# A hybrid recurrent and attention block: the attention output projection by token halves, inputs scaled as they are split, the embedding projection moved, the score heads alternated

## What is computed

```
h = rmsnorm(x, g_mix);  z = h @ w_in            # lx, lg, q, k, v
y_lru = rmsnorm(rg_lru(conv(lx)) * gelu(lg), g_lru_out)
y_att = rmsnorm(chunk_window_attention(q, k, v, sinks), g_attn_out)
x = x + concat([y_lru, y_att]) @ w_out
h = rmsnorm(x, g_ffn)
x = x + square(relu(h @ w_ff1)) @ w_ff2         # d_ff = 4096
gate = sigmoid(rmsnorm(x, g_ple) @ w_ple_gate)
x = x + gate * (p @ w_ple_proj)                 # p is 1024 x 256
return rmsnorm(x, g_final)
```

## Time and profile before

| | |
|---|---|
| median of 3 runs | 1165.95 us (1165.94 to 1166.27) |
| the profiled execution | 1165.31 us |
| its span in the profile | 1163.5 us |
| mean granted TensorE clock | 0.987 of full |
| PE / DVE / ACT / POOL busy | 1120.2 / 690.1 / 363.8 / 397.4 us |

### The profile page before, as it was taken

How to read it: one execution, slowest core, us unless ns; L and a number is a source line. 1 busy time by engine, 2 the same in 40 slices (tenths; PEclk the granted TensorE clock), 3 DMA queues, 4 the chain that set the end, 5 groups by cost and what they waited for, 6 DMA issues and landing times.

```text
span 1163.5 us, 13983 instructions
## 1 busy us (share of the span) xinstructions
PE 1120.2 (96%) x5196; PEld 922.9 (79%) x5196; DVE 690.1 (59%) x869; ACT 363.8 (31%) x597; POOL 397.4 (34%) x207
## 2 busy tenths in 40 slices
...
DMA packets 22481, 69.43 MB, mean 60 GB/s; under 512 B 2352, under 2 KB 4400, under 8 KB 22448
## 3 DMA queue, kind: packets, MB, share of 16 engines
...
## 4 chain that ended last, share of the span: by engine, by line
PE 83%; DVE 12%; issue 2%; POOL 1%; ACT 1%; DMA 1%; SPq 0%; DVEq 0%; ACTq 0%
PE bank L460 27%; PE bank L461 26%; PE bank L462 26%; DVE h_lo L1042 4%; DVE r_mix L1047 1%; DVE xT L1271 1%; PE bank L550 1%; DVE lane L1094 1%; DVE scaled L1269 1%; PE bank L579 1%; POOL gx_lo L397 1%; PE bank L508 1%; PE bank L564 1%; DMA stage<-in_w_in 1%; POOL w_lo L368 1%
## 5 line engine op out<-in xcount | busy, mean ns | idle before, releaser
L460 PE MATMUL bank<-h_hi,w_hi 128*128 128x512 f32 (+1 forms) x1056 | 408.9, 387 | 25.2 <-DVE h_lo L1042 16.1
L461 PE MATMUL bank<-h_lo,w_hi 128*128 128x512 f32 (+1 forms) x1056 | 401.7, 380 | 0.0
L462 PE MATMUL bank<-h_hi,w_lo 128*128 128x512 f32 (+1 forms) x1056 | 401.4, 380 | 0.0
L430 POOL TENSOR_TENSOR w_lo<-stage,w_hi 128x1024 fp32r<-128x1024 f32 x64 | 152.7, 2409 | 524.6 <-ACT w_hi L940 524.6
L1319 DVE TENSOR_TENSOR xT<-bank,xT 128x512 f32<-128x512 f32 x256 | 176.3, 691 | 142.6 <-PE bank L462 142.3
L460 PEld LDWEIGHTS bank<-h_hi,w_hi 128*128 128x128 f32 x1056 | 201.7, 191 | 72.1 <-issue 10.2
L461 PEld LDWEIGHTS bank<-h_lo,w_hi 128*128 128x128 f32 x1056 | 202.0, 191 | 37.4 <-issue 1.6
L462 PEld LDWEIGHTS bank<-h_hi,w_lo 128*128 128x128 f32 x1056 | 201.5, 191 | 37.7
L460 PE MATMUL bank<-u_hi,w_hi 128*128 128x512 f32 x512 | 199.2, 389 | 0.0
L461 PE MATMUL bank<-u_lo,w_hi 128*128 128x512 f32 x512 | 199.2, 389 | 0.0
L462 PE MATMUL bank<-u_hi,w_lo 128*128 128x512 f32 x512 | 199.2, 389 | 0.0
...
## 6 DMA issues: line engine op xcount, KB each, us to landing
...
out_x<-o_ring SPq DMA_DIRECT2D x7, 256.0 KB, 2.2
...
```

The lines of the kernel that those rows point to most:

```text
L430: pool.tensor_tensor(w_lo[:, n0 % 2, o:o + HP], stage[:, s0 % STAGES, :], w_hi[:, n0 % 2, o:o + HP], ALU.subtract).then_inc(w_split, 1)
L460: pe.matmul(o, whi, hh, start=first, stop=False)
L461: pe.matmul(o, whi, hl, start=False, stop=False)
L462: return pe.matmul(o, wlo, hh, start=False, stop=last)
```

## The change

- **Score heads alternated.** `scores(u)` issued the four matmuls of key/value head 0 (channels on partitions 0 to 63, bank 4) and then the four of head 1 (partitions 64 to 127, bank 5). It now issues head 0, head 1, head 0, head 1, and both heads' outputs are signalled at the end.
- **Attention output projection by token halves.** Stage 3 now does all 8 output tiles of token half 0, then those of half 1, so both weight pieces are needed by the fifth group, and piece 9 is free only after group 12. 
- **Its inputs scaled when split.** `att_norm` (VectorE, one instruction per tile, L1159's form) multiplies attention outputs by gain and 1/rms; `att_high` copies (ScalarE), `att_low` subtracts (VectorE); `add_a` is one VectorE instruction. For this the sum of squares of half 0 is moved forward: GpSimd adds it after `probs(6)` and before `probs(7)`, ScalarE squares in unit 5, and TensorE's `sum_rows(SS_ATT)` stands in unit 6 behind `turn_p(6)` instead of behind unit 7's groups.
- **The feed-forward's inputs scaled when split.** `ffn_norm` (VectorE, 16 instructions) applies gain and 1/rms, `ffn_split` (ScalarE) copies, and the 16 subtractions move from VectorE to GpSimd (`ffn_low`). `hidden`'s relu no longer multiplies. VectorE adds the squares of half 1 (GpSimd did). The first `ff1` waits for the sum of squares, root and reciprocal of its token half; its half 1 goes by input tiles with both outputs in step. It waits for `main_free` A0+15 (bank 0, `add_a(14)`) and A0+16.
- **Embedding projection moved.** All 8 outputs of part 0 are computed right after the last `ff2`, ScalarE copies them to `kept` in SBUF, and the gates of part 0 follow without projections between them. The embedding weights come by two transfers on ScalarE's queue in stage 3 instead of through SyncE's stage ring, and are split by ScalarE and VectorE in the first feed-forward block instead of by ScalarE and GpSimd after the last.

```diff
             if n < IN_PIECES:
                 eng.wait_ge(main_done, 4 * (n + 1))
+            elif n < IN_PIECES + 2:
+                eng.wait_ge(main_done, L0 + 8 * (n - IN_PIECES + 1))
             else:
-                eng.wait_ge(main_done, IN_GROUPS + 8 * (n - IN_PIECES + 1))
+                eng.wait_ge(main_done, A0 + 12 + 4 * (n - IN_PIECES - 2))
...
+                if u == 6:
+                    sums(SS_ATT, sq, acc)
             low(2 * 10)
             low(2 * 10 + 1)
             sums(SS_FFN, sq, acc)
+
+            def ffn_low(k, hf):
+
+                pool.wait_ge(ffn_high, KD * hf + k + 1)
+                pool.tensor_tensor(h_lo[:, k, half(hf)], raw_h(k, hf), h_hi[:, k, half(hf)], ALU.subtract
+                                   ).then_inc(ffn_ready, 1)
+
+            for k in range(4):
+                ffn_low(k, 0)
             low(2 * FF_FIRST)
             low(2 * FF_FIRST + 1)
-            sums(SS_FFN + 1, sq, acc)
+            for k in range(4, KD):
+                ffn_low(k, 0)
+            for k in range(KD):
+                ffn_low(k, 1)
...
                 pe.wait_ge(main_free, IN_GROUPS - (0 if u >= UNITS // 2 else 2))
-                for g in range(NKV):
-                    if u >= 1:
-                        pe.wait_ge(s_read, 2 * (u - 1) + g + 1)
-                    else:
-                        pe.wait_ge(rms_done, SS_LRU + 2)
-                    r = slice(g * HD, (g + 1) * HD)
-                    for cp in range(2):
-                        c = 2 * u + cp
-                        for a in range(2):
+                if u >= 1:
+                    pe.wait_ge(s_read, 2 * u)
+                else:
+                    pe.wait_ge(rms_done, SS_LRU + 2)
+                for cp in range(2):
+                    c = 2 * u + cp
+                    for a in range(2):
+                        for g in range(NKV):
+                            r = slice(g * HD, (g + 1) * HD)
                             last = pe.matmul(bank[4 + g][:, (2 * cp + a) * P:(2 * cp + a + 1) * P],
                                              qT[r, c, 2 * a:2 * a + 2, :].rearrange("p a q -> p (a q)"),
                                              kT[r, c * CHUNK:c * CHUNK + P], start=True, stop=True)
-                    last.then_inc(s_done, 1)
+                            if cp == 1 and a == 1:
+                                last.then_inc(s_done, 1)
...
-                if u == UNITS - 1:
-                    pe.wait_ge(s_read, 2 * UNITS)
-                    sum_rows(SS_ATT, acc, 4)
+                        if u == UNITS - 2:
+                            pe.wait_ge(s_read, 2 * UNITS)
+                            sum_rows(SS_ATT, acc, 4)
                 values(u)
             for g in range(A_GROUPS):
-                n, hf, m = g // 8, (g % 8) // 4, g % 4
+                hf, n, m = g // 8, (g % 8) // 4, g % 4
                 if g == 3:
                     pe.wait_ge(o_read, UNITS)
                 group(A0 + g, IN_PIECES + 2 + n, LT, m, hf, LT, H_ATT + 4 * hf if n == 0 and m == 0 else None,
-                      g % 8 == 0)
-                if g == 4:
+                      hf == 0 and m == 0)
+                if g == 1:
                     sum_rows(SS_ATT + 1, acc, 5)
-                if g == 14:
+                if g == 8:
                     sum_rows(SS_FFN, acc, 7)
...
+            pe.wait_ge(w_split, 2 * (FF_FIRST + 1))
             for hf in range(2):
-                pe.wait_ge(h_ready, ffn_number(KD - 1, hf) + 1)
                 for m in range(2):
-                    pe.wait_ge(main_free, MAIN_GROUPS - 1 + hf)
-                    ff1(0, hf, m)
-                    if hf == 1 and m == 0:
+                    pe.wait_ge(relu_done, 2 * hf + m + 1)
+                pe.wait_ge(main_free, A0 + (15, 16)[hf])
+                for k, m in ([(k, m) for m in range(2) for k in range(KD)] if hf == 0 else
+                             [(k, m) for k in range(KD) for m in range(2)]):
+                    if m == 0:
+                        pe.wait_ge(ffn_ready, KD * hf + k + 1)
+                    c = k * 256 + m * P
+                    last = passes(bank[2 * hf + m][:, :], w_hi[:, n1, c:c + P], w_lo[:, n1, c:c + P],
+                                  h_hi[:, k, half(hf)], h_lo[:, k, half(hf)], k == 0, k == KD - 1)
+                    if k == KD - 1:
+                        last.then_inc(ff1_done, 1)
+                    if hf == 0 and m == 0 and k == 5:
                         sum_rows(SS_FFN + 1, acc, 7)
...
...
+            for m in range(KD):
+                project(0, m)
+            pe.wait_ge(y_added, 4 + 16 * FF_BLOCKS)
+            sum_rows(SS_PLE, acc2, 4)
             for part in range(len(PARTS)):
                 for i in range(GATE_PIECES):
                     for m in range(2):
                         gate(part, i, m)
-                        if part == 0 and i == 0 and m == 0:
-                            pe.wait_ge(y_added, 4 + 16 * FF_BLOCKS)
-                            sum_rows(SS_PLE, acc2, 4)
-                    for m in range(2):
-                        project(part, 2 * i + m)
+                    if part >= 1:
+                        for m in range(2):
+                            project(part, 2 * i + m)
...
+                if u == 5:
+                    for j in range(LT):
                         square(SQ_BY[SS_ATT] - 4 + j, sq, q_tile(j, 0))
-            root(SS_ATT, 4, r_mix, ATT)
+                if u == 6:
+                    root(SS_ATT, 4, r_mix, ATT)
+                if u == 7:
+                    att_high(0)
             act.wait_ge(o_read, UNITS)
-            for j in range(LT):
-                split_high(H_ATT + 4 + j, q_tile(j, 1), v_att[:, j:j + 1], LT + j, 1)
             for j in range(LT):
                 square(SQ_BY[SS_ATT + 1] - 4 + j, sq, q_tile(j, 1))
             piece_free(act, 8)
             high(2 * 10)
             high(2 * 10 + 1)
             root(SS_ATT + 1, 5, r_mix, ATT)
+
+            def ffn_split(k, hf):
+
+                act.wait_ge(ffn_normed, KD * hf + k + 1)
+                act.activation(h_hi[:, k, half(hf)], raw_h(k, hf), ACT.Copy).then_inc(ffn_high, 1)
+
+            def ffn_square(k, hf):
+                act.wait_ge(main_free, A0 + 8 * hf + k + 1)
+                square(SQ_BY[SS_FFN + hf] - 8 + k, sq, xT[:, k, half(hf)])
+
+            for k in range(2):
+                ffn_square(k, 0)
+            att_high(1)
             act.dma_start(pT[:, :, :], p.rearrange("(k q) t -> q k t", q=P)).then_inc(p_in, 16)
-
...
+            for k in range(2, KD):
+                ffn_square(k, 0)
+            act.wait_ge(h_ready, H_PLE)
+            for h in range(2):
+                act.dma_start(pw_raw[:, h * HP:(h + 1) * HP], w_ple_proj[0, h]).then_inc(pw_in, 16)
+            ffn_square(0, 1)
+            root(SS_FFN, 7, r_ffn, D)
+            ffn_square(1, 1)
             for k in range(4):
-                ffn_square(k, 0)
-                ffn_high(k, 0)
+                ffn_split(k, 0)
+                if k % 2 == 1:
+                    ffn_square(2 + k // 2, 1)
             piece_free(act, 9)
             high(2 * FF_FIRST)
             high(2 * FF_FIRST + 1)
-            for k in range(4):
-                ffn_high(k, 1)
             for k in range(4, KD):
-                ffn_square(k, 0)
-                ffn_high(k, 0)
-            for k in range(4):
+                ffn_split(k, 0)
+                if k == 5:
+                    ffn_square(4, 1)
+            for k in range(5, KD):
                 ffn_square(k, 1)
-            root(SS_FFN, 7, r_ffn, D)
-            for k in range(4, KD):
-                ffn_high(k, 1)
-                ffn_square(k, 1)
+            root(SS_FFN + 1, 7, r_ffn, D)
+            for k in range(KD):
+                ffn_split(k, 1)
...
+            def ple_high(k, hf):
+                act.wait_ge(y_added, 4 + 16 * (FF_BLOCKS - 1) + KD * hf + k + 1)
+                split_high(H_PLE + KD * hf + k, xT[:, k, half(hf)], v_ple[:, k:k + 1], k, hf)
+                square(SQ_BY[SS_PLE + hf] - 8 + k, sq2, xT[:, k, half(hf)])
+
+            def keep(m):
+                act.wait_ge(ple_done, m + 1)
+                act.activation(kept[:, m, :], bank[m % 4][:, :], ACT.Copy).then_inc(pp_kept, 1)
 
...
-            ple_high(0)
-            project_high()
+            for k in range(KD):
+                ple_high(k, 0)
+            keep(0)
+            keep(1)
             act.wait_ge(ff2_done, 16 * FF_BLOCKS)
-            gate_high(GATE_FIRST + 2)
+            gate_high(GATE_FIRST + 1)
+            for k in range(6):
+                keep(2 + k)
+                ple_high(k, 1)
             root(SS_PLE, 4, r_mix, D)
-            ple_high(1)
+            for k in range(6, KD):
+                ple_high(k, 1)
...
+            def att_norm(hf):
+
+                for j in range(LT):
+                    dve.wait_ge(sq_done, SQ_BY[SS_ATT + hf] - 3 + j)
```

(77 more changed lines are left out.)

124 lines of the change are left out of this document (57 added, 67 removed).

## The result

After the change the kernel takes 1171.76 us, the median of five runs (1171.3 to 1172.01), against 1165.95 before (five runs now, 1163.19 to 1167.52): 1.0051 of the time before, with a 95% interval of 1.0036 to 1.0066. It is slower, by 5.8 us; the forecast was 1162.5. The profiled execution took 1172.01 us with a span of 1170.2, 6.7 more than the span before.

What follows compares the result with a forecast made beforehand. TensorE, busy 96% of the span, was taken as the bound. Terms -3.2 + 4.5 + 1.7 + 3.9 - 10.3 = -3.4 on 1165.3 gave 1161.9, with 0.6 for the median 1162.5 us; range 1152 to 1172.

Steps and rivals of the forecast that it cites:

- The gates' part 0: Stretch after the last `ff2`: with projections moved ahead of the gates it falls from 66.9 to 56.6 us, -10.3 us.
- The wait for half 0's sum in unit 6: Attention unit 6: TensorE waits for ScalarE's squares and GpSimd's copy and adds of them, +4.5 us.
- everything moves together: Premise in attention unit 6: shorter scores shift all engines' work there alike, leaving the 4.5 us wait unchanged.
- The scores: Attention units: alternated heads share the array, 0.63 us less per group; five groups (scores 3 to 7) count, -3.2 us.
- rival B: Attention scores: the heads don't share the array, so the first edit does nothing; +3.2, 1165.7 us, chance 0.12.
- I count these two: Stage 3, half 0's chain: of 14 VectorE instructions only two meetings, with GpSimd's 1024-column weight lows, cost time: 4.4 us.
- The 47.3 without meetings: Stage 3: half 0's chain, through `add_a(14)`, ends at 47.3 us if no VectorE instruction meets GpSimd.
- GpSimd's short lows: Stage 3: 512-column lows come in pairs with gaps, partly over while ScalarE squares; no meetings with them counted.
- From half 1's sum to `ff2`: Feed-forward start: root, reciprocal, scaling, copy, eight GpSimd lows and two weight lows take 24.1 us, to `ff2` at 82.5.
- the term that stood at +3.9: Start of stage 3 to the first `ff2`: 82.5 us against 78.6, +3.9 us, bounds -5 and above +12.
- One loss of 1.7 us: Lower clock behind the new waits in unit 6 and ahead of `ff2`, counted once for both: +1.7 us (0 to 3.4).
- Rival A: Stage 3: VectorE and GpSimd take turns throughout, chain ends at 60, clock falls at both waits; 1172.3 us, chance 0.21.

## Why the prediction was wrong

The sum said 3.4 us less on the profiled execution, and it became 6.7 more, a miss of 10.1 us.

**Right.** The gates' part 0: -10.3 said, -10.6 measured, and the same 56.21 us when done alone. The wait for half 0's sum in unit 6: 4.5 said; TensorE stood still for 5.2 (252.96 to 258.15), for the reason given: ScalarE's squares and GpSimd's adds of them. One premise of it did not hold: when the scores get shorter, not everything moves together. `turn_p(6)` came 3.0 us earlier and ScalarE only 1.9, which made the wait longer by 1.1; the adds, 1.41 us apart and not 1.54, took 0.4 off. The scores: 0.63 us each said, 0.55 in every unit of the trace after, 2.75 for the five. That the units lose 3.3 in the run with this edit alone, near the 3.2, is partly luck: the other 0.5 is the clock, whose lower level lasts 5.0 us behind `values(0)` there and 5.9 before. Heads do share the array: the two heads' matmuls start within 0.01 us of each other, a pair every 0.11 us. So rival B is out. The Trainium skill (TensorEngine Tiling (Array Packing), Overview) gives up to twofold for two row tiles; the measured ratio is 1.64 to 1.09, 1.5. Before, one matmul started every 0.11 us, but three pairs ran together already, where head 1's began behind head 0's.

**The step that failed: "I count these two".** The start of `ff1` was put at 47.3 + 4.4 = 52 us in stage 3, with two meetings of VectorE with GpSimd's weight lows. It was 55.6. The 47.3 without meetings was right (47.5 with GpSimd idle), so what failed is the count of the meetings. GpSimd's short lows stood at nothing, because they come in pairs with gaps and are partly over while ScalarE squares. They cost 5.0 us: 1.0 in the second pair of scalings, 1.0 in the first of the third, 2.0 in the fourth pair and 0.9 in one more add. The two weight lows were met as said, by the second scaling of the third pair and the add behind it, but cost 2.1 + 0.8 = 2.9 us and not 4.4. The 4.4 was mis-sized from the rows themselves: it takes the whole 2.25 us of a VectorE instruction beside such a low, where the loss is what it has above 0.67, 1.6, so 3.2 for two. The error on one side hid part of that on the other. The Trainium skill (SBUF — State Buffer, SBUF: two separate sides) describes an exclusive lock on a shared port pair; this trace agrees, down to the add with one input in PSUM that was not held up.

**From half 1's sum to `ff2`**, 24.1 said, 26.2 measured. GpSimd's eight short lows took 1.65 us each, all beside VectorE, where five had been counted so: 1.0 of the 2.1. Its weight lows took 0.4 more than said. They ended at 360.05 as the last but one; the last was VectorE's `u_lo`, which met them, and the start behind it makes up the rest. The lines of both engines:

```profile
339.82 10.58 DVE L1337 SCALAR_TENSOR_TENSOR raw<-xT,vec,r_ffn 128x512 f32<-128x512 f32 x8
...
355.70 2.15 DVE L1377 TENSOR_TENSOR usq<-relu 128x512 f32<-128x512 f32 x1
357.89 2.71 DVE L1381 TENSOR_TENSOR u_lo<-usq,u_hi 128x512 fp32r<-128x512 f32 x1
```

```profile
341.32 13.20 POOL L431 TENSOR_TENSOR h_lo<-raw,h_hi 128x512 fp32r<-128x512 f32 x8 [13.86 <-ACT h_hi L946]
354.48 5.57 POOL L447 TENSOR_TENSOR w_lo<-stage,w_hi 128x1024 fp32r<-128x1024 f32 x2
```

With the sum of half 1 coming 5.8 us behind `ff1`'s start instead of 6.4, the three differences are 3.6 + 2.1 - 0.6 = 5.1: +9.0 us for the term that stood at +3.9.

**The clock.** One loss of 1.7 us was counted for two new waits. The first `ff2` lost 2.7, and of the units' 4.3 some 2.4 are left when the 5.2 us of standing still are taken out and the 3.3 of the scores put back: 5.1 in all, 3.4 more than said and outside the 0 to 3.4 that the prediction gave. In the trace the lower level lasts 6.0 us behind the sum of half 0, which is 3.0 lost, and a little comes back behind `values(0)`. That size is not the change's alone: the last section shows the same wait with less behind it.

**The rest**, 1.3 us, is the 0.65 at either end. The edits do not touch what lies there, and it differs as much between the other traces of this study: `values(0)` starts between 200.9 and 202.7 us, and the last stretch takes 74.4 to 76.0. No cause in the change can be read from it. With 0.7 for the wait in unit 6, 0.1 back from the scores (the 3.3 of the run with them alone) and 0.3 from the gates, 5.1 + 3.4 + 1.3 + 0.7 - 0.1 - 0.3 = 10.1.

Rival A named the right place. That its time, 1172.3, is within 1 us of the measured one is luck: it has +12 and 3.4 where +9.0 and 5.1 came, and the 1.3 of the two ends was in nobody's sum. It wanted `ff1` at 60, and `ff1` at 55.6 lies just below the 56 from which A was said to decide. The range, 1152 to 1172, held the time at its very edge.

**What was not asked.** The largest number of the study was in no term: scaling at the split puts root, reciprocal and eight scalings of either half ahead of `ff1`, where before only the relu waited for root and reciprocal and no scaling existed. Taken back, with the division of work around it, it gives 20 us. The prediction priced this chain only against the kernel before, where `ff1` waited anyway; with the token halves and the feed-forward unscaled `ff1` starts at 46 us.
